# A two-block transformer kernel: index key and index weights in one projection tile, six selection rounds and the low halves in another place

## What is computed

```python
proj = h @ w_in                      # q 1024, k 256, v 256, qi 512, ki 64, wi 8 columns
q = _rope(_rmsnorm(q, q_norm_g), positions)
k = _rope(_rmsnorm(k, k_norm_g), positions)
qi = _rope(qi, positions)
ki = _rope(_layernorm(ki, idx_k_ln_g, idx_k_ln_b)[:, :, None, :], positions)[:, :, 0, :]
wi = wi * (IDX_HEADS ** -0.5 * IDX_DIM ** -0.5)
# for each block of 128 queries:
s = jnp.einsum('bqhd,bsd->bqhs', qib, ki)
score = jnp.einsum('bqhs,bqh->bqs', jax.nn.relu(s), wib)
score = jnp.where(causal[None], score, -jnp.inf)
_, sel = lax.top_k(score, topk)      # topk = 128
# attention of 16 query heads on 4 key heads over the selected keys, softmax
return o @ w_out
```

## Time and profile before

| | us |
|---|---|
| median of 3 runs | 2109.09 (2108.90 to 2109.94) |
| the profiled execution | 2109.04 |
| its span in the trace | 2106.9 |
| second mixer: first_two and projection, in the trace | 930.6 to 1061.9 |
| its attention | 1061.9 to 1157.0 |

### The profile page before, as it was taken

The page is one execution under the profiler, slowest core; times in us unless marked ns, Lnnn a source line. Parts: engine busy times, 40 slices in busy tenths (PEclk is TensorE's granted clock), DMA queues, the critical chain, the costliest instruction groups (busy, mean ns, idle before and its releaser), DMA issues.

```text
span 2106.9 us, 28195 instructions
## 1 busy us (share of the span) xinstructions
PE 2089.5 (99%) x9944; PEld 1715.2 (81%) x9944; DVE 1248.7 (59%) x1844; ACT 787.0 (37%) x1091; POOL 298.8 (14%) x357
## 2 busy tenths in 40 slices
PE   9999999999999999999999999999999999999999
PEld 8888888887888888877767888888888888888887
DVE  7666544787676654465996676654466456333332
ACT  6222333547442223344366442223343234222222
POOL 0122400650212230024300212210000000000000
PEclk9999999999999999999999999999999999999999
DMA  5565333320345642323310346542333222222232
GB/s 193 181 194 196 93 110 111 118 94 2 110 162 188 200 136 83 96 96 116 101 31 1 104 157 198 184 145 81 96 106 108 93 90 100 100 93 97 76 96 87
DMA packets 79571, 243.31 MB, mean 115 GB/s; under 512 B 12784, under 2 KB 13424, under 8 KB 79376
## 3 DMA queue, kind: packets, MB, share of 16 engines
q1 hardware_dynamic: 61376, 189.61, 27.6%
q0 software_dynamic: 18128, 52.84, 8.0%
HBM read 235.84 MB, written 2.29 MB: 113 GB/s over the span
## 4 chain that ended last, share of the span: by engine, by line
PE 91%; DVE 6%; ACT 1%; issue 1%; DMA 1%; SPq 0%; ACTq 0%; DVEq 0%
PE ps L710 28%; PE ps L712 28%; PE ps L711 28%; PE ps L1009 2%; DVE ps L1979 2%; PE ps L991 1%; PE ps L970 1%; DVE tmp L1623 1%; DVE small L1877 1%; PE ps L1133 0%; DVE ropA L1850 0%; DVE qA L1852 0%; PE ps L741 0%; DMA w_raw<-in_up 0%; PE ps L728 0%
## 5 line engine op out<-in xcount | busy, mean ns | idle before, releaser
L710 PE MATMUL ps<-h_hi,w_hi 128*128 128x512 f32 x1888 | 740.1, 392 | 1.4 <-DVE h_lo L1922 0.9
L712 PE MATMUL ps<-h_hi,w_lo 128*128 128x512 f32 x1888 | 734.9, 389 | 0.0
L711 PE MATMUL ps<-h_lo,w_hi 128*128 128x512 f32 x1888 | 734.8, 389 | 0.0
L1580 DVE TENSOR_TENSOR w_lo<-w_raw,w_hi 128x1024 fp32r<-128x1024 f32 x336 | 411.5, 1226 | 384.7 <-ACT w_hi L1216 370.3
L1216 ACT ACTIVATE w_hi<-w_raw 128x1024 fp32r<-128x1024 f32 x383 | 402.3, 1052 | 242.7 <-PE ps L712 240.6
L710 PEld LDWEIGHTS ps<-h_hi,w_hi 128*128 128x128 f32 x1888 | 353.6, 187 | 82.4 <-issue 7.5
L712 PEld LDWEIGHTS ps<-h_hi,w_lo 128*128 128x128 f32 x1888 | 353.6, 187 | 75.5
L711 PEld LDWEIGHTS ps<-h_lo,w_hi 128*128 128x128 f32 x1888 | 353.7, 187 | 72.8 <-issue 0.2
L710 PE MATMUL ps<-hid_hi,w_hi 128*128 128x512 f32 x704 | 273.9, 389 | 0.0
L711 PE MATMUL ps<-hid_lo,w_hi 128*128 128x512 f32 x704 | 273.9, 389 | 0.0
L712 PE MATMUL ps<-hid_hi,w_lo 128*128 128x512 f32 x704 | 273.9, 389 | 0.0
(11 more groups left out here) (309 smaller groups left out, 1760.1 us busy)
## 6 DMA issues: line engine op xcount, KB each, us to landing
ada_raw<-in_ada_w POOLq DMA_DIRECT2D x96, 512.0 KB, 4.9
w_raw<-in_gate SPq DMA_DIRECT2D x88, 512.0 KB, 3.5
w_raw<-in_up SPq DMA_DIRECT2D x88, 512.0 KB, 3.3
w_raw<-in_down SPq DMA_DIRECT2D x64, 384.0 KB, 3.1
w_raw<-in_down SPq DMA_DIRECT2D x64, 320.0 KB, 2.8
w_raw<-in_w_mix_c SPq DMA_DIRECT2D x24, 512.0 KB, 3.2
w_raw<-in_w_mix_b SPq DMA_DIRECT2D x17, 512.0 KB, 3.4
w_raw<-in_w_mix SPq DMA_DIRECT2D x16, 512.0 KB, 3.2
```

The costliest lines, as they stand in the source:

```text
L710: pe.matmul(dest, s_hi, m_hi, start=first and n == 0, stop=False)
L711: pe.matmul(dest, s_hi, m_lo, start=False, stop=False)
L712: mm = pe.matmul(dest, s_lo, m_hi, start=False, stop=last and n == len(pairs) - 1)
L1580: dve.tensor_tensor(chunk(w_lo, slot, WT), chunk(w_raw, slot, WT), f32(chunk(w_hi, slot, WT)), ALU.subtract).then_inc(w_lo_done, 1)
```

## The change

Four things, in the second mixer only.

1. **One tile for key and weights.** The tile ki holds the key once (columns 0 to 63), wi (columns 64 to 71) and 56 empty columns. The tile wi is gone, so there are 17 jobs; `first_two` makes ki and qi0, and qi0's bias is added as wi's was. The key's operations cover 64 rows. The second copy of the key, which the index scores of every second head read, is made by one more transfer before the four of the swap, and the swapped copies all read rows 0 to 63.
2. **The key's steps.** Its spread is in the second gap of step 4 (before: first gap of step 5), its rope in step 5 (before: 6), after that step's qi rope. All index gaps are half a step earlier, counted in m. qi's ropes come one step earlier with their tiles, the swaps of qi one load less behind their tile.
3. **Rounds.** 27 of the 48 rounds are in the projection, 21 in the attention, by the table `TOPS_IN_PAIRS`: one in slot 5, one in most slots from 7 on, two in slots 16, 19 and 22.
4. **Low halves.** For the twelve groups of blocks 0 to 2, ScalarE copies the turned output from PSUM to `ropB` as well, and GpSimd makes the low half from this copy. TensorE's turn of the next group waits for that copy and not for the low half.

```diff
-        TILES_B = ["ki", "wi", "qi0", "qi1", "qi2", "qi3", "vB0", "vB1", "kB0", "kB1"] + [f"qB{t}" for t in range(8)]
+        TILES_B = ["ki", "qi0", "qi1", "qi2", "qi3", "vB0", "vB1", "kB0", "kB1"] + [f"qB{t}" for t in range(8)]
...
-            return tmp[:, 3 * T + s * P:3 * T + s * P + (8 if n == 3 and s == 1 else P)]
+            return tmp[:, 3 * T + s * P:3 * T + (s + 1) * P]
...
-                return 6
+                return 5
...
+        def low_by_pool(group):
+            return group[0] == "b" and first_pair(group)[2] < TT - 1
+
+        def kept_turned(group):
+            at = (GROUPS.index(group) % 2) * T
+            return ropB[:, at:at + 2 * P]
...
-        TOPS_AT = {8: (0, 1), 9: (4, 1), 10: (5, 2), 11: (4, 1), 12: (0, 2), 13: (3, 0), 14: (3, 0), 15: (3, 0), 16: (3, 0),
-                   17: (1, 0)}
+        TOPS_AT = {8: (0, 4), 9: (1, 4), 10: (1, 3), 11: (1, 0), 12: (1, 0), 13: (3, 0), 14: (3, 0), 15: (3, 0), 16: (3, 0)}
+        TOPS_IN_PAIRS = {5: 1, 7: 1, 8: 1, 9: 1, 10: 1, 11: 1, 12: 1, 13: 1, 14: 1, 15: 1, 16: 2, 17: 1, 18: 1, 19: 2, 20: 1, 21: 1,
+                         22: 2, 23: 1}
...
-            at = 4 * (m - 6) + 2 * part - 2
-            return IDX[max(at, 0):at + 2] if 0 <= at < len(IDX) else []
+            at = 4 * (m - 6) + 2 * part
+            return IDX[at:at + 2] if 0 <= at < len(IDX) else []
...
+                if t == "ki":
+                    sp.dma_start(kraw[HD:P, :], kraw[0:HD, :]).then_inc(rot_sem(t)[0], 16)
...
+            def turned_lows():
+
+                for group in GROUPS:
+                    if low_by_pool(group):
+                        after(pool, g_kept, group)
+                        to, _ = group_places(True, group)
+                        high, _ = group_places(False, group)
+                        kept = kept_turned(group).rearrange("p (k t) -> p k t", k=2)
+                        pool.tensor_tensor(to, kept, f32(high), ALU.subtract).then_inc(g_low.at(group), 1)
...
-                if G >= 1:
+                if G >= 1 and low_by_pool(GROUPS[G - 1]):
+                    after(pe, g_kept, GROUPS[G - 1])
+                elif G >= 1:
...
-                if part == 0 and m == 5:
+                if part == 1 and m == 4:
                     head_spread("ki")
...
+                if low_by_pool(group):
+                    if group == ("b", 0):
+                        after(act, h_roped, "qB7")
+                    before = [g for g in GROUPS[:GROUPS.index(group)] if low_by_pool(g)]
+                    if len(before) >= 2:
+                        after(act, g_low, before[-2])
+                    act.activation(kept_turned(group), bank(7)[:, 0:2 * P], ACT.Copy).then_inc(g_kept.at(group), 1)
...
+            after(act, d_misc, "qi_scaled")
+            act.activation(straight("qi0"), straight("qi0"), ACT.Identity, bias=shift_out(3, 1)).then_inc(h_scaled.at("qi0"), 1)
             lead(J + 1)
...
-                    if u >= 6 and u % 2 == 0:
+                    if u >= 6 and u % 2 == 0 and not low_by_pool(group_of(pairs[u - 6])):
                         group_low(group_of(pairs[u - 6]))
...
+            dve.tensor_tensor(straight("qi0"), bank(1), ssum[:, :], ALU.mult).then_inc(d_misc.at("qi_scaled"), 1)
```

130 lines of the change are left out of this document (74 added, 56 removed).

## The result

Over 20 runs of each, the changed kernel took 2112.45 us (2109.37 to 2118.47) and the kernel before 2108.85 us (2107.41 to 2115.13). The ratio is 1.0016, 95% interval [1.0009, 1.0023]: some 3.4 us longer, within the 0.2% that the prediction called no change, but 7.6 us above its 2104.9 and outside its range. The profiled execution took 2116.62 us for a span of 2114.7.

What follows compares the result with a forecast made beforehand. TensorE, busy 99% of the span, was taken as the bound. The terms -5.44 - 0.5 - 1.2 + 0.65 + 1.5 + 0.8 gave -4.2 us, so 2104.9 us from 2109.09, range 2102.3 to 2107.5.

Steps and rivals of the forecast that it cites:

- The tile: Second mixer's projection: one job of 24 matmuls goes from TensorE at 0.227 us each, -5.44 us.
- The spread of 4 products: Index key's spread on TensorE: 4 products instead of 8 take half of 1.09 us, -0.5 us.
- The shift sum: TensorE's wait at line 752 grows because the sum needs 128 columns, not 8: +0.65 us, bounds 0.1 and 0.96.
- The key's wait: First index scores: TensorE's wait for the key's rope goes, since the rope comes a step earlier, -1.2 us.
- the spread's wait: Index key's spread: TensorE waits for a reciprocal queued on VectorE behind both qi ropes, +1.5 us (0.6 to 2.1).
- The moved rounds in the projection: VectorE does 27 rounds there instead of 33; they lay beside matmuls with no TensorE wait, so 0 us.
- The attention: Rounds added and low halves removed on VectorE, after idle time and cover: net +0.8 us, bounds -1.6 and +3.
- The sum from slot 16 to 24: Attention slots 16 to 23, VectorE: 11 rounds instead of 6 (+7.0) less four low halves, +5.7 us.
- the lead of 1.6 us at slot 16: Attention up to slot 15: narrower rounds and fewer low halves, less mask and diagonal add, put VectorE 1.6 us earlier.
- a cover of 1.1: Attention: before the change, pair 24's exponential was ready 1.1 us before TensorE needed it (1123.85 against 1124.91).
- the rounds bound the attention: Rival: doubled rounds in slots 16, 19 and 22 delay exponentials, attention +3 instead of +0.8, 2107.1 us; chance 0.2.
- The slower rival: Rival: GpSimd's low halves hold up VectorE's scaled maxima, up to +8.9 us, 2113.8 us; decides past 0.35 us each; chance 0.05.

Runs made afterwards that it cites:

- i1: g2 with one selection round moved from slot 22 to slot 3, where VectorE was idle: 2106.81 us, ratio 0.9986 to the kernel before.
- h3: The kernel before with the six moved rounds and the low halves on GpSimd, key and weights still in two tiles: 2112.72 us, ratio 1.0018.
- h2: The changed kernel with idle matmuls filling three TensorE waits (shift sums, ahead of the attention, slot 26): 2112.47 us; profile at full clock throughout.
- f5: The kernel before with only the six selection rounds moved into the attention: 2113.92 us, ratio 1.0027.
- f2: The kernel before with only the low halves made by GpSimd from ScalarE's copy: 2108.97 us, ratio 0.9999.
- g4: The changed kernel with the attention's 21 rounds in earlier slots: one each in 2 to 6, two in 7, one each in 8 to 21: 2115.29 us.
- g1: The changed kernel with 14 selection rounds per query block instead of 16, so six fewer in the attention (112 keys picked, not 128): 2111.57 us, ratio 1.0006.
- g2: The changed kernel with two VectorE orders changed: key spread's reciprocal ahead of a rope, first key tile's normed product ahead of four rounds: 2109.50 us, ratio 1.0004.
- h4: g2 with the six rounds back in the projections (33 there, 15 in the attention): 2112.13 us, ratio 1.0015.
- f3: The kernel before with only the packed key-and-weights tile, 33 rounds in the projections, low halves on VectorE: 2120.91 us, ratio 1.0053.
- f1: The changed kernel with the low halves back on VectorE, packed tile and moved rounds kept: 2113.71 us, ratio 1.0014.
- i3: f2 with four idle matmuls ahead of the last sum of squares before the attention: 2109.26 us, ratio 0.9994.

## Why the prediction was wrong, step by step

- **The tile, -5.44 us**: right. The two kernels' profiles differ by 8 x 3 product instructions there, and with the waits mended (i1) the projection is 5.2 us shorter, 0.7 of it by the key's wait, which is 0.5 there and not 1.2. But at the end of the kernel little of it arrives: against h3, which has the other two parts without the packing, the changed kernel is 1.5 us faster at equal clock.
- **The spread of 4 products, -0.5 us**: wrong, it gives nothing. The row that answers to line 941 of the earlier trace rows:

```profile
963.38 1.09 PE L972 MATMUL ps<-identity,hrB 128*64 128x128 f32 x8 [1.63 <-DVE hrB L1875]
```

Eight instructions take 1.09 us, as sixteen did: the products for the two halves of 64 columns had run side by side (in the trace of before they start in pairs, 6 to 7 ns apart). The Trainium skill, page "TensorE: Matmul & The Clock Gate", section "Part 3: Packing small matmuls — row/col tiling", says that small matmuls in different parts of the array run at the same time. The two rows agree, and I had divided a duration by a count instead.
- **The shift sum, +0.65 us**: mis-sized. The wait grew from 0.9 to 1.9 us here, to 1.8 to 2.1 in the other packed profiles without fills. That is the upper bound of 0.96 and a little more.
- **The key's wait, -1.2, and the spread's wait, +1.5 us**: right; the second measured 1.6.
- **The moved rounds in the projection, 0**: failed. I counted only that six rounds leave. Of those that stay, four stand in step 9 ahead of the first key tile's norm, and TensorE waits 1.0 us for it in the next tile's spread. In the kernel before no such wait is listed. I had not read in VectorE's new order what stands between this norm and its rounds.
- **The projection as a whole**: 2.9 us shorter. The tile and the key's wait less the two waits at the spreads make 4.0. Of the other 1.1 us, which are in no wait of the list, 0.6 are in the key's own small work, now 64 rows or columns wide: from the product ahead of it to a product behind it, its mean takes 1.88 us where it took 1.55, its sums of squares 1.30 where they took 1.03. The rest is not placed.
- **The attention, +0.8 us**: failed, it is +3.3 (83.1 to 86.4 at full clock), outside both ranges that I gave it (-1.6 to +3, and -0.5 to +2 among the open terms). The sum from slot 16 to 24 held: 11 rounds for 6 less four low halves, +5.7, and the maximum of pair 24 came 28.8 us after that of pair 16 instead of 25.1, after 2 to 2.4 us of idle time were used up. What was not there is the lead of 1.6 us at slot 16: counted from the first score, the maximum of pair 16 came at 34.37 us instead of 34.51, a lead of 0.1. VectorE's maxima of pairs 0, 16 and 24 in h2 (first score at 1058.09):

```profile
1060.08 0.42 DVE L1938 TENSOR_REDUCE small<-ps 128x2 f32<-128x256 f32 x1
...
1092.46 0.95 DVE L1938 TENSOR_REDUCE small<-ps 128x2 f32<-128x768 f32 x1
...
1121.27 1.23 DVE L1938 TENSOR_REDUCE small<-ps 128x2 f32<-128x1024 f32 x1
```

and in before (first score at 1061.25):

```profile
1062.62 0.42 DVE L1877 TENSOR_REDUCE small<-ps 128x2 f32<-128x256 f32 x1
...
1095.76 0.95 DVE L1877 TENSOR_REDUCE small<-ps 128x2 f32<-128x768 f32 x1
...
1120.83 1.22 DVE L1877 TENSOR_REDUCE small<-ps 128x2 f32<-128x1024 f32 x1
```

VectorE began the attention 0.6 us behind (first maximum 1.99 us after the first score, before 1.37). The single parts show where the lead went. The rounds, masks and diagonal were to give 0.3 of it (1.1 less 0.8), and f5 has a lead of 0.07: the tenth round, counted as free in slot 5, found only 0.6 us of idle time more to fill. The low halves were to give 1.3, and f2 has a lead of 0.3: the five of them are gone (2.1 us of VectorE's time, 1.65 by the prediction's 0.33 each), but the scaled maxima beside GpSimd's take 1.3 us more (16 x 79 ns). The scaled maxima from the first score to the maximum of pair 16, in before (1061.25 to 1095.76) and then in f2 (1059.98 to 1094.19):

```profile
L1880 DVE TENSOR_TENSOR small<-small,qnsB 128x2 f32<-128x2 f32 x16 | 2.6, 161 | 0.6
L1912 DVE TENSOR_TENSOR small<-small,qnsB 128x2 f32<-128x2 f32 x16 | 3.8, 240 | 0.6
```

With the lead gone, pair 24's maximum came 3.6 us late against a cover of 1.1. The path failed too: I had TensorE wait first, and only, for the exponentials of pair 24. In h2 the score of pair 18 is where it was before, counted from the first score, that of pair 19 is 1.0 us late (a wait of 0.9 for exponentials, behind the two rounds of slot 16), that of pair 22 1.55 and that of pair 26 3.25, the last step being the norm that stands behind pair 24's maximum. This is the rival "the rounds bound the attention" (+3), which I gave 0.2. Its doubled rounds show in the wait at pair 19, but doubling is not what it takes: g4, with one doubled slot, costs as much. f5 and g1 show the price from two more sides.
- **The slower rival**, GpSimd's hold-ups: its mechanism is there, at 0.13 us for each of the twelve low halves of the 0.35 needed (0.25 for each of the first five). It did not decide alone, but it took most of the lead that the low halves were to give. The Trainium skill, page "SBUF — State Buffer", section "SBUF: two separate sides", has the rule of the shared port, and the rows of f2 and before above bear it out for a line of two columns.
- **The granted clock**: in none of my cases. It makes the difference between 2109.7 us at full clock and the median of 2112.45. Of the new waits, those at the shift sums and at slot 26 (1.5 to 2.1 us) cost their own length and in several profiles 3.4 us at half clock behind them, 1.7 us more in full work.

At full clock: -2.9 for the projection, +0.9 to 1.0 for the shift sum, +3.3 for the attention make +1.3 us. Measured were 1.3 to 1.8. The rest of the 3.6 us between the medians is clock.

## What to carry to other kernels

Where a saving shortens a stage that covers another engine's work, count that engine's whole queue from its first dependent step to each of its deadlines; moving its work to a later place saves nothing if it is busy there too. A new wait of TensorE can cost more than its length, through the clock. First look for idle places of the covering engine and for small results that stand behind long ones in its queue: here two changed orders and one moved round turned +0.16% into -0.14%.

## What the runs showed of the hardware

The granted clock went to 1.2 GHz behind some short standstills of TensorE, and not behind others of the same length. Of the ten profiles in which TensorE waited 1.79 us or more for the shift sums, with full work on both sides, four have 3.4 us at half clock right behind it; of the eight with 1.2 us or less none has. Of the seven with a standstill of 1.4 to 1.9 us at slot 26, six have it (all but g2); of those without, none has one there. The waits of 2.57 us in g4, 3.26 in h4, 2.8 and 2.1 in f3, and 2.68 near 459 us in f1 and i3 were all followed by it. But of the seven with a wait of 1.6 to 1.7 us at the key's spread none has it there, and f5 and f1 have none behind 1.4 us at pair 19. So a wait's length alone does not tell; what else decides is open. f1, f2 and g1 have 3.4 us at the attention's start, where no wait is over 0.7 us. Stretches of 10 us and more are there too: one of 20.5 us in two profiles at the attention's start, one of 10.2 us behind 1.15 us at pair 4 (i3), and one of 10 to 14 us behind the 1.2 us at the end of the attention in three of eighteen profiles, all of which have that wait. What makes those stays open: filling the wait ahead of the attention did not make them rarer.

What the half clock costs depends on the work: in the changed kernel the 20.5 us at the attention's start put the maximum of pair 16 5.7 us later than in h2, the 3.4 us behind slot 26 cost 1.7.
